# Written-out chunk loops, dot products between variance and root, and rows spread ahead of a V block in a transformer-layer kernel

## What is computed

```python
def one(xc):                                   # 128 tokens
    q = (xc @ wq).reshape(PEER_CHUNK, PEER_HEADS, 2, PEER_DKEY // 2)
    s = jnp.einsum('nhpd,hpkd->nhpk', q, subkeys)
    ...                                        # two top-16 lists per head, 16 best sums: idx, top_s
    g = jax.nn.softmax(top_s, axis=-1)
    act = jax.nn.gelu(jnp.einsum('nhkd,nd->nhk', u[idx], xc))
    return jnp.einsum('nhk,nhkd->nd', g * act, v[idx])
...
x_mid = x + g1 * rmsnorm(mix_x, g_post_mix)
hx2 = modulate(rmsnorm(x_mid, g_pre_ffn), sh2, sc2)
x = x_mid + g2 * rmsnorm(peer(hx2, ...), g_post_ffn)
```

## Time and profile before

| | us |
|---|---|
| median of 3 runs | 3514.86 |
| lowest, highest run | 3506.70, 3516.95 |
| the profiled execution | 3502.35 |
| its span | 3500.6 |
| TensorE busy, VectorE busy | 2738.6 (78%), 2201.0 (63%) |
| GpSimd busy, ScalarE busy | 1967.9 (56%), 776.7 (22%) |
| `v` slots on TensorE (L1456) | 1414.1 |
| dot products on VectorE (L1126) | 1230.9 |
| gathers on GpSimd (L436) | 987.3 + 960.6 |

### The profile page before, as it was taken

One profiled execution on the slowest core, in us unless ns is written; L12 is line 12 of the kernel. 1 busy time (PEld: TensorE's weight loads), 2 busy tenths in 40 slices (PEclk: granted clock), 3 DMA queues, 4 the chain that ended last, 5 costly groups with the idle time before them and its releaser, 6 DMA issues.

```text
span 3500.6 us, 37036 instructions
## 1 busy us (share of the span) xinstructions
PE 2738.6 (78%) x9084; PEld 1156.4 (33%) x9084; DVE 2201.0 (63%) x4614; ACT 776.7 (22%) x1791; POOL 1967.9 (56%) x2100
## 2 busy tenths in 40 slices
PE   7998876266977887789779977897789778934498
PEld 3775343143232323232323233323332333211122
DVE  2224942898876767676766676767676766766500
ACT  1122531021221222122212222122212221200122
POOL 0000000366776767676767676767666666677775
PEclk9999888588988999899889988998899898976799
DMA  6003240499999999999999999999999999999998
GB/s 233 31 21 118 99 165 9 156 360 372 387 390 374 398 367 403 367 397 373 390 375 396 370 393 383 392 381 376 383 393 381 358 387 388 377 408 402 400 394 349
DMA packets 327018, 1146.04 MB, mean 327 GB/s; under 512 B 37357, under 2 KB 41453, under 8 KB 325624
## 3 DMA queue, kind: packets, MB, share of 16 engines
q0 software_dynamic: 295552, 1075.97, 79.4%
q1 hardware_dynamic: 31224, 67.38, 5.3%
HBM read 1134.83 MB, written 8.39 MB: 327 GB/s over the span
## 4 chain that ended last, share of the span: by engine, by line
PE 43%; DMA 24%; issue 13%; DVE 12%; POOL 5%; ACT 2%; POOLq 0%; DVEq 0%; SPq 0%; ACTq 0%
PE psum L1456 26%; DMA arena<-in_v,arena 13%; DMA arena<-in_u,idx_u 11%; POOL arena L436 5%; DVE arena L1126 4%; PE psum L1280 4%; PE psum L1411 4%; PE psum L1337 2%; PE psum L1389 2%; PE psum L1263 2%; PE psum L1376 1%; PE psum L1266 1%; PE psum L1229 1%; DVE small L1001 1%; DVE arena L944 1%
## 5 line engine op out<-in xcount | busy, mean ns | idle before, releaser
L1456 PE MATMUL psum<-arena 128*32 128x512 f32 x4096 | 1414.1, 680 | 334.8 <-DMA arena<-in_v,arena 327.9
L1126 DVE CUSTOM_DVE_ANT_0 arena<-arena,psum 128x1024 f32<-128x1024 f32 x1024 | 1230.9, 1219 | 512.6 <-DMA arena<-in_u,idx_u 480.4
L436 POOL DMA_INDIRECT arena<-in_v,arena x1024 | 987.3, 964 | 448.7 <-issue 241.9
L436 POOL DMA_INDIRECT arena<-in_u,idx_u x1024 | 960.6, 938 | 438.0 <-issue 218.2
L1456 PEld LDWEIGHTS psum<-arena 128*32 128x32 f32 x4096 | 390.9, 120 | 1303.8 <-issue 834.1
L695 ACT ACTIVATE arena<-arena 128x32 f32<-128x32 f32 x1024 | 317.0, 320 | 1488.0 <-PE psum L1456 1475.4
L1337 PE MATMUL psum<-kT,arena 64*128 64x512 f32 (+1 forms) x384 | 184.8, 622 | 72.4 <-ACT arena L626 35.3
L1411 PE MATMUL psum<-wbig,arena 128*128 128x512 f32 x512 | 230.6, 605 | 2.2 <-ACT arena L664 2.2
L1357 PE MATMUL psum<-ident,arena 128*128 128x128 f32 x640 | 119.5, 312 | 80.3 <-DVE arena L1015 44.3
L1369 PE MATMUL psum<-arena,v 128*64 128x128 f32 x1280 | 163.0, 285 | 22.7 <-ACT arena L637 22.7
L1369 PEld LDWEIGHTS psum<-arena,v 128*64 128x64 f32 x1280 | 147.6, 144 | 37.9 <-ACT arena L637 34.1
(11 more groups left out here) (199 smaller groups left out, 1999.0 us busy)
## 6 DMA issues: line engine op xcount, KB each, us to landing
wbig<-in_w_mod SPq DMA_DIRECT2D x8, 2048.0 KB
arena<-in_u,idx_u POOLq DMA_INDIRECT x1024, 6.5
arena<-in_v,arena POOLq DMA_INDIRECT x1024, 6.6
arena<-in_w_mod SPq DMA_DIRECT2D x4, 2048.0 KB, 8.9
wbig<-in_wq SPq DMA_DIRECT2D x1, 8192.0 KB, 34.6
arena<-in_xin SPq DMA_DIRECT2D x5, 1024.0 KB, 5.1
wbig<-in_w_in SPq DMA_DIRECT2D x2, 2048.0 KB, 21.8
arena<-in_w_out SPq DMA_DIRECT2D x1, 4096.0 KB, 15.1
```

The lines of the kernel that those rows point to most:

```text
L436: pool.indirect_dma_start(ring[:, r, :], None, t[table], bass.IndirectOffsetOnAxis(idx[:, j:j + 1], 0)).then_inc(got[r], 16)
L1126: V.tensor_tensor_reduce(ring[:, r, :], ring[:, r, :], hx_cur, 1.0, 0.0, ALU.mult, ALU.add, act_[:, j:j + 1]).then_inc(S["u_used"], 1)
L1456: ins = M(bank(4 + b)[QP * q:QP * q + QP, :], lhsT=sel[:, j % SELS, :], rhs=ring[:, r, 512 * b:512 * b + 512], start=(i == 0), stop=(i == ...
```

## The change

Four things, and nothing else.

1. The loops over chunks of GpSimd, ScalarE, VectorE and TensorE are written out: the same six passes, with constants in the place of registers. The loop over token pairs ahead of them and the loop on the queue of stores (SyncE) stay.
2. Two semaphores that counted "opened" gathers, and that nothing waits for, are no longer raised for each gather.
3. On VectorE the mixing norm's variance comes after dot product 83, not 82; two more dot products stand between that variance and its reciprocal, and two between the second norm's.
4. On TensorE the rows A2 and B2 are spread one after the other; four `v` slots that stood between them (`fill(ROWS_AT + 1)`) come behind both, ahead of the transposes. On ScalarE the weight columns that stood ahead of the second square are four fewer (`cols(ROWS_AT)`).

```diff
-MIX_AT, XM_AT, GATES_AT = 82, 88, 10
+MIX_AT, XM_AT = 83, 88
...
                 freed(c, u_place(c, j))
-                pool.sem_inc(S["u_opened"], 1)
                 gather("u", idx_u, j, u_place(c, j) % RING)
...
                 freed(c, v_place(c, j))
-                pool.sem_inc(S["v_opened"], 1)
                 gather("v", idx_v, token(j), v_place(c, j) % RING)
...
-            with pool.Fori(0, NX - 2) as k:
-                ch.enter(k, 4)
-                mixed_gathers(k)
-                lead_gathers(k + 1)
-            ch.leave(NX - 2)
-            mixed_gathers(NX - 2)
-            lead_gathers(NX - 1)
+            for c in range(NX - 1):
+                mixed_gathers(c)
+                lead_gathers(c + 1)
...
-                cols(ROWS_AT + 1)
+                cols(ROWS_AT)
                 act.wait_ge(S["xm_ready"], n + 1)
...
-                if not isinstance(n, int):
+                if n >= 3:
                     act.wait_ge(S["ff_free"], n - 1)
...
-            with act.Fori(0, NX - 2) as k:
-                ch.enter(k, 1)
+            for k in range(NX - 2):
...
                 fill(MIX_AT)
                 variance(n + 1, 48, "mix_sq", "mix_var")
+                fill(MIX_AT + 2)
                 rstd(n + 1, 48, "mix_sd")
...
                 fill(XM_AT)
                 variance(n + 1, 48, "xm_sq", "xm_var")
+                fill(XM_AT + 2)
                 rstd(n + 1, 48, "xm_sd")
...
-            with dve.Fori(0, NX - 2) as k:
-                ch.enter(k, LOOP_STEPS)
+            for k in range(NX - 2):
...
                 spread(2, A2, "a2_ready")
-                fill(ROWS_AT + 1)
                 spread(0, B2, "b2_ready")
                 fill(HXT_AT)
...
-            with pe.Fori(0, NX - 2) as k:
+            for k in range(NX - 2):
```

More of the change, by code:

```diff
@@ L74 @@
 IN_FIRST = (11, 11, 11, 7)
-MIX_AT, XM_AT, GATES_AT = 82, 88, 10
+MIX_AT, XM_AT = 83, 88
 PAIR_STEPS = 31
-LOOP_STEPS = 183
 class Chain:
```

## The result

| | before | changed |
|---|---|---|
| median of 4 runs, us | 3510.78 | 3409.22 |
| lowest to highest | 3505.16 to 3516.95 | 3407.63 to 3413.81 |
| ratio (95% interval) | | 0.9712 (0.9690 to 0.9735) |
| the profiled execution, its span | 3502.35, 3500.6 | 3407.63, 3405.9 |
| instructions executed | 37036 | 29441 |

The kernel is faster by 101.6 us, 2.9%. The median before has one run more than the three known at the forecast, which is why it is 3510.78 here and 3514.86 there. A pass now takes 339 to 343 us (from one copy of the `u` indices on GpSimd to the same copy one chunk later) and not 356, where 347 to 348 was forecast.

The account below looks back on a forecast made before the run. The prediction took the stream of gathers, at 409 GB/s, as the bound, with holes of some 28 us a pass. Loops 21.5 us plus norms 24 us made 45.5 us off 3514.86, so 3469 us, range 3435 to 3497.

Parts of the forecast that it names:

- The step that failed: GpSimd's gathers: removing register instructions and some 1792 semaphore raises gains nothing, its step being 0.03 us under the stream's.
- Rival D: GpSimd's gathers: waiting on the gather itself lengthens its step; slower, 3595 for 0.10 us more; chance 0.05.
- the sum: Whole kernel: 21.5 us from the loops plus 24 us from the norms, 45.5 us faster.
- The jumps' term: Starts of passes: five jumps back go away, 4.3 us of stream each, 21.5 us in all.
- the loop's entry: First pass's start, reached without a jump back: its 380 GB/s, against 341 at the repeats, measured a jump's cost.
- VectorE's jump counts nothing: VectorE's loop over chunks: its jump lies beside TensorE's and GpSimd's and adds no gain.
- Rival A: Starts of passes: the standstill is fetch of new code and stays; only the norms gain, 3491; chance 0.08.
- The norms: Norms of six passes: reordered work gains 4.0 us of the 7.6 lost each time, 24 us in all.
- B2 after A2 would take 2 to 3.8 us more: TensorE at the norms: spreading B2 behind A2's 3.78 us adds 2 to 3.8 us before the four slots.
- rival C: Norms and jumps: more comes back, the norms' whole loss and 6.8 us per jump, 80 us, 3435; chance 0.06.
- The 28 us of stream lost in a pass: Each 356 us pass: some 28 us of stream lost beyond a chunk's 328 us of gathers at 409 GB/s.
- the two places that I had explained: The norms and the way from one pass to the next, said to hold more than half of each pass's loss.

Follow-up runs that it names:

- e13: Changed kernel with the semaphore raises put back between each gather's wait and the gather: 3451.96 us, 0.9831 of the kernel before.
- e14: Changed kernel with the same raises put back, but one line higher, ahead of each gather's wait: 3413.47 us, 0.9716 of the kernel before.
- e15: Changed kernel with the loop over chunks back on TensorE alone: 3441.59 us, 0.9797 of the kernel before.
- e7: Changed kernel with the loop over chunks back on GpSimd alone, together with its semaphore raises: 3460.89 us, 0.9852 of the kernel before.
- e16: Changed kernel with the loop over chunks back on VectorE alone: 3416.95 us, 0.9734 of the kernel before.
- e6: Changed kernel with the norms as before, so loops written out and raises gone only: 3431.89 us, 0.9768 of the kernel before.
- e5: The changed kernel itself, run again where the kernel before takes 3514 us: 3413.04 us, 0.9717 of the kernel before.
- e1: Changed kernel with the norms as before, on the slower chip: 0.9728 of the kernel before.
- e9: Changed kernel with the loop over chunks back on TensorE alone, on the slower chip: 0.9687 of the kernel before.
- e10: Changed kernel with the loop over chunks back on VectorE alone, on the slower chip: 0.9644 of the kernel before.
- e12: Changed kernel with the 2048 semaphore raises put back between wait and gather, on the slower chip: 0.9863 of the kernel before.

## Why the prediction was wrong

**The step that failed: "The register instructions that go count nothing either: the stream waits for buffers. The same holds for the 1792 or so semaphore raises that GpSimd loses: its step is already 0.03 us under the stream's."** The raises cost 38.5 us (e13 against e14). The step compared rates: GpSimd's 1.25 us against the stream's 1.28. But the first half of the sentence, that the stream waits for buffers, is the reason why a rate was the wrong measure. Where GpSimd waits for a buffer, what counts is the time from its release to the next gather, and the raise lay in it with 0.54 us. The row that shows it was in the trace of the kernel before: the gather at 1461.34 follows this read-out, which ended at 1460.53.

```profile
1460.45 0.08 DVE L1126 DVE_READ_ACCUMULATOR2_ANT arena<- 128x1 f32 x1
```

I read its 6.55 us of idle time and not the 0.81 us at its end. Rival D had the right place and the wrong sign; it moved the wait onto the gather and asked only whether the gather's step would grow. It did not: the usual step is 1.24 us with and without. That the forecast has the right direction is no merit of this step: the sum had nothing for the raises, and the other terms alone made it.

**The jumps' term, 21.5 us, was mis-sized.** TensorE's loop costs 28 us (e15), GpSimd's 47.9 - 38.5 = 9.4 us by e7 and e13 (two sessions), VectorE's 3.5 (e16, not told from nothing): 41 us, register instructions and their fetch included. With the raises that is 79.4 of the 82.4 us that e6 shows, if costs measured one at a time add up, which no run tests. I took the loop's entry (380 GB/s) as the measure of "no jump". The repeats of the changed kernel have 395, but its entry has 380 still (922 to 967 us), and e13's entry, with the raises, 385: the entry is a slower place by itself, jumps and raises or not, and no measure for the repeats. With 395 in its place the term would have been 5.9 us a jump, 30 us. That VectorE's jump counts nothing held within the noise; for ScalarE's only the slower chip speaks.

**Rival A** (the standstill is fetch of new code and stays) is refuted by the changed profile: no "issue" of over 1 us ahead of the scores or of the copy of the indices, at any of the starts. What the Trainium skill says in Runtime: NRT & Kernel Launch, Instruction fetch mechanics, held in kind: straight code ran without a standstill, and with the jump back TensorE stands 23.5 us in all (e15). The Trainium skill's 108 ns for a compare-and-branch (Advanced Engine Details and Errata, Control Flow Timing) is not what a jump cost here: its five standstills in e15 are 4.6 to 4.7 us each.

**The norms.** 24 us were forecast, 18.9 measured (e5 against e6). The mechanism came out almost by the number: the variance stays and the reciprocal comes at once; GpSimd stands 2.12 and 2.62 us (2.3 and 3.5 forecast); the transposes 12.4 us after `xm` (12.7). The windows gained 5.2 us a pass, of which e6 gives the norms the 4.0 that were forecast; but of these six times 4.0 us, 24, only 18.9 reached the end. The item that was wrong is that B2 after A2 would take 2 to 3.8 us more: the two run in pairs, and both together took 3.79. The slots behind them so began 3.7 us after A2's start and not 7.8, and GpSimd's second stand is shorter by about 1 us than forecast.

**The range** ended at 3435 with rival C, "more comes back than I count", at a chance of 0.06. The 28 us of stream lost in a pass, six times 28 = 168 us, stood in the first paragraph and would have allowed 100. I took as bounds only the two places that I had explained, at which 60 of the 101.6 us came back.

## What to carry to other kernels

Where a ring of buffers feeds a saturated stream, look at the time from a buffer's release to the next request, not only at the requester's rate: here an instruction between the wait and the request took 0.54 us of each turn that was waited for, 38.5 us in all, and one line higher nothing that could be seen. A jump back in a hardware loop cost 28 us on the engine whose first work others wait for, and nothing clear of noise where it lay in a wait. And when explained places hold half of a loss, the bound for a change that touches the whole program is the whole loss.

## What the runs showed of the hardware

- A semaphore raise on GpSimd between a wait and an indirect gather delays the gather by 0.54 us (0.81 against 0.27 us from the release); the gap between gathers whose wait has long passed is 0.30 us in both cases. The kernel lost 38.5 us by it (e13 against e14).
- 7600 more instructions on the otherwise waiting SyncE slowed the kernel by 13.4 us; they are 60 more packets on an instruction queue. How much of it is fetch on shared DMA engines and how much the raises' own doing wasn't separated; SyncE's own transfers went out as before.
- The same kernel took 3510 to 3514 us in four sessions and 3861 to 3869 in two, with a mean granted clock of 0.84 to 0.86 for 0.87 to 0.89, and the slices' rate down by about a tenth (e1, e9, e10 and e12 have 346 to 359 GB/s in the mean of the tenth to the 39th, the same four kernels here 394 to 398). The ratios did not all keep their order: the kernel with TensorE's loop (0.9676, 0.9687) is faster there than the one with the norms as before (0.9728) and slower here (0.9797 for 0.9768), though the intervals there overlap. The raises cost more there (2.2% for 1.1%).
- Matmuls of one row over 128 partitions, from two different rows (A2 and B2), ran in pairs on TensorE when they stood one behind the other: eight in 3.79 us, at a granted clock of 0.50, where four of one row took 3.78 us at the same clock. Each pair begins within 0.014 us, in all eight places of the changed kernel.
- A jump back left TensorE standing 4.6 to 4.7 us in each of five passes (e15) and GpSimd 3.1 to 4.4 us (e7); in the written-out code neither stands.
